# Two-layer hybrid diffusion trunk on one core: adaLN's bias, a fourth weight tile, and the order of the conditioning tiles

## What is computed

```python
def adaln(cvec, w, b):
    m = jax.nn.silu(cvec) @ w + b
    return jnp.split(m[:, None, :], N_MOD, axis=-1)
...
h = modulate(rmsnorm(xp, norm_mix[l]), sh1, sc1)   # h*(1+sc1)+sh1
xp = xp + g1 * mixer(h)
xp = xp + g2 * moe(modulate(rmsnorm(xp, norm_ffn[l]), sh2, sc2))
```

## Time and profile before

| what | us |
|---|---|
| median of 3 runs (1729.19 to 1732.13) | 1731.81 |
| the profiled execution | 1730.03 |
| its span, first to last instruction | 1728.2 |
| PE busy | 1591.8 (92%) |
| DVE busy | 639.7 (37%) |
| ACT busy | 375.8 (22%) |
| POOL busy | 73.6 (4%) |

### The profile page before, as it was taken

One profiled execution on the slowest core, in us unless ns is written; L12 is line 12 of the kernel. 1 busy time (PEld: TensorE's weight loads), 2 busy tenths in 40 slices (PEclk: granted clock), 3 DMA queues, 4 the chain that ended last, 5 costly groups with the idle time before them and its releaser, 6 DMA issues. The chain is left out here.

```text
span 1728.2 us, 23854 instructions
## 1 busy us (share of the span) xinstructions
PE 1591.8 (92%) x9359; PEld 783.6 (45%) x9423; DVE 639.7 (37%) x1350; ACT 375.8 (22%) x700; POOL 73.6 (4%) x118
## 2 busy tenths in 40 slices
PE   4999997999999999999699877889999999999993
PEld 1335546444444444444244345464444444444441
DVE  1124423433333333333315364224333333343333
ACT  1102313112222222221310143121222221221221
POOL 2200000000000000000102033000000000000000
PEclk9999998999999999999899988879999999999996
DMA  9876937799999999998537300178999999999970
GB/s 341 285 292 238 379 104 319 285 399 389 390 389 394 393 399 386 392 382 364 211 136 219 97 13 13 40 304 326 400 383 390 396 395 380 398 392 391 393 293 37
DMA packets 106318, 524.02 MB, mean 303 GB/s; under 512 B 8965, under 2 KB 10160, under 8 KB 54688
## 3 DMA queue, kind: packets, MB, share of 16 engines
q1 hardware_dynamic: 101392, 510.06, 75.5%
q0 software_dynamic: 4880, 13.33, 2.3%
HBM read 518.01 MB, written 2.23 MB: 301 GB/s over the span
## 5 line engine op out<-in xcount | busy, mean ns | idle before, releaser
L903 PE MATMUL bank<-big 128*64 128x512 f32 x2112 | 464.5, 592 | 1.7 <-issue 1.7
L903 PEld LDWEIGHTS bank<-big 128*64 128x64 f32 x2112 | 152.4, 137 | 301.5 <-issue 301.5
L925 PE MATMUL bank<-big 128*64 128x512 f32 x1056 | 241.1, 598 | 1.0 <-DVE big L1526 1.0
L577 PE MATMUL bank<-big,hT 128*128 128x512 f32 (+1 forms) x544 | 233.1, 590 | 7.7 <-ACT hT L1032 5.1
L892 PEld LDWEIGHTS bank<-onehot,big 128*128 128x128 bf16 x3168 | 177.7, 98 | 53.1 <-issue 53.1
L892 PE MATMUL bank<-onehot,big 128*128 128x128 bf16 x3168 | 198.6, 219 | 0.0
L1148 ACT ACTIVATE big<-bank,sl 128x512 bf16<-128x512 f32 x132 | 90.7, 687 | 425.7 <-PE bank L925 425.7
L934 PE MATMUL bank<-big,back 128*128 128x512 bf16 x728 | 171.2, 384 | 9.7 <-DVE big L1544 6.1
L1538 DVE SCALAR_TENSOR_TENSOR xn<-bank,sl,big 128x512 f32<-128x512 f32 x132 | 99.1, 751 | 182.0 <-ACT big L1148 182.0
L577 PEld LDWEIGHTS bank<-big,hT 128*128 128x128 f32 x544 | 104.6, 193 | 133.4 <-issue 123.1
L1518 DVE TENSOR_TENSOR big<-big,bank 128x256 f32<-128x256 f32 x66 | 27.9, 422 | 278.2 <-ACT big L1142 278.2
(11 more groups left out here) (274 smaller groups left out, 1095.5 us busy)
## 6 DMA issues: line engine op xcount, KB each, us to landing
big<-in_w_gate_dram SPq DMA_DIRECT2D x132, 1024.0 KB, 9.3
big<-in_w_up_dram SPq DMA_DIRECT2D x132, 1024.0 KB, 11.2
big<-in_w_down_dram SPq DMA_DIRECT2D x132, 1024.0 KB, 9.0
big<-in_w_ada_dram SPq DMA_DIRECT2D x24, 2048.0 KB, 11.4
big<-in_w_in_rec_dram SPq DMA_DIRECT2D x8, 2048.0 KB, 12.6
big<-in_w_in_attn_dram SPq DMA_DIRECT2D x4, 2048.0 KB, 8.1
big<-in_w_out_attn_dram SPq DMA_DIRECT2D x2, 2048.0 KB, 11.1
big<-in_w_out_rec_dram SPq DMA_DIRECT2D x2, 2048.0 KB, 9.8
```

The costliest lines, as they stand in the source:

```text
L577: mm = pe.matmul(bk[:, 0:w.shape[2]], hT[:, c, g * P:(g + 1) * P], w[:, c, :], start=(c == 0), stop=(c == KC - 1))
L903: mm = pe.matmul(gub[CAP * q:CAP * (q + 1), :], hg[:, j, c, CAP * q:CAP * (q + 1)], gu_slot[2 * j + q][:, :, c, :], start=(c == 0), stop=( ...
L925: mm = pe.matmul(yb[half][CAP * q:CAP * (q + 1), :], hsT[:, f, CAP * q:CAP * (q + 1)], d_slot[2 * j + q][:, f, half * 512:(half + 1) * 512 ...
```

## The change

The bias product goes away, with `dup` and `bias24`. Layer 0's gates get their bias from rows broadcast to all partitions (`brow`, two loads of 1024 values to 128 partitions) when they are evicted; layer 1's kept gates get theirs on DVE instead of ACT's copy; the modulations get theirs from a small table `bmod` (eight loads of 4 KB) by one scalar_tensor_tensor in every ada_mod. Tile 3 gets a place outside the ring (`first4`), so that SP issues it without a wait, and tiles 4, 5 and 6 wait for tiles 0, 1 and 2; from tile 7 on the rule is n-3 as before. The large part of the constants is issued after tile 4 instead of after tile 3. In MID each projection tile goes before its filter job, filtw goes behind the fourth, nab before the fifth and spec behind it. In ATT one ada tile stands ahead of the first scores, each later one comes one unit earlier, and mod and keep move to odd units.

```diff
-    out["dup"] = ...
...
-    MID = [("filt", 0), ("in", 0), ("ada", 4), ("ada", 5)] + [("gate", i) for i in range(4)]
-    MID += [("filt", 1), ("in", 1), ("ada", 6), ("ada", 7), ("mod", 2)]
-    MID += [("filt", 2), ("in", 2), ("ada", 8), ("ada", 9), ("mod", 3), ("filtw", 0), ("filtw", 1)]
-    MID += [("in", 3), ("ada", 10), ("ada", 11)] + [("gate", i) for i in range(4, 8)]
-    MID += [("spec", 0), ("spec", 1), ("spec", 2), ("nab", 0), ("nab", 1), ("in", 4)]
+    MID = [("in", 0), ("filt", 0), ("ada", 4), ("ada", 5)] + [("gate", i) for i in range(4)]
+    MID += [("in", 1), ("filt", 1), ("ada", 6), ("ada", 7), ("mod", 2)]
+    MID += [("in", 2), ("filt", 2), ("ada", 8), ("ada", 9), ("mod", 3)]
+    MID += [("in", 3), ("filtw", 0), ("filtw", 1), ("ada", 10), ("ada", 11)] + [("gate", i) for i in range(4, 8)]
+    MID += [("nab", 0), ("nab", 1), ("in", 4), ("spec", 0), ("spec", 1), ("spec", 2)]
...
-    ATT = []
+    ATT = [("ada", 0)]
     for u in range(NU + 2):
         ATT += [("s", u)] if u < NU else []
         ATT += [("t", u - 1)] if 0 <= u - 1 < NU else []
         ATT += [("v", u - 2)] if 0 <= u - 2 else []
-        ATT += [PAIRS[u // 2 - 1]] if u % 2 == 0 and u >= 2 else []
-        ATT += [("ada", u)] if u < N_ADA else []
+        ATT += [PAIRS[u // 2]] if u % 2 == 1 and u < N_ADA else []
+        ATT += [("ada", u + 1)] if u + 1 < N_ADA else []
...
+        SLOT = [0, 1, 2, 3] + [(n - 4) % 3 for n in range(4, len(order))]
+        BEFORE = [max([m for m in range(n) if SLOT[m] == SLOT[n]], default=None) for n in range(len(order))]
...
-                    if n >= 3 and n - 3 not in early:
-                        sp.wait_ge(mm_done, tile_job[n - 3] + 1)
+                    if BEFORE[n] is not None and BEFORE[n] not in early:
+                        sp.wait_ge(mm_done, tile_job[BEFORE[n]] + 1)
...
-                    if n == 3:
+                    if n == 4:
                         sp.dma_start(cst[:, early_cst:], ...
...
+            for l in range(2):
+                for i, v in enumerate((0, 1, 3, 4)):
+                    pool.dma_start(bmod[:, l, i, :], ...).then_inc(gain_in, 16)
...
             pool.wait_ge(mod_ready, 1)
+            for i, v in enumerate((2, 5)):
+                pool.dma_start(brow[i], row(A["b_ada"][0, v * D:(v + 1) * D], D)).then_inc(brow_in, 16)
+            pool.wait_ge(row_zero, 1)
...
+                    pool.dma_start(bkeep[r:r + G, :], ...).then_inc(bkeep_in, 16)
...
-                    pe.matmul(..., stop=(c >= KC - NT and q > 0))
-                pe.wait_ge(bada_in, 16)
-                pe.wait_ge(cst0_in, 16)
-                pe.matmul(bk[0:ROWS, :], cs("dup", ...), bias24, start=False, stop=True).then_inc(mm_done, 1)
+                    mm = pe.matmul(..., stop=(c >= KC - NT))
+                mm.then_inc(mm_done, 1)
...
-                    if kind == "keep":
-                        bk = take(act, J["keep", u, 1])
-                        act.activation(gsave[r, :], bk[r, :], ACT.Copy).then_inc(ev_done, 1)
...
+                    dve.tensor_tensor(gates[:, g, i // 4, c], bk[:, :], brow[i // 4][:, c], ALU.add).then_inc(ev_done, 1)
...
+                dve.wait_ge(gain_in, 16 * 12)
+                drained(dve, j + 1)
+                link(dve.scalar_tensor_tensor(out=m, in0=m, scalar=float(i % 2), in1=bmod[:, l, i, :]..., op0=ALU.add, op1=ALU.add))
                 if i % 2:
-                    link(dve.tensor_scalar(mod[:, l, i, :, :], mod[:, l, i, :, :], 1.0, None, ALU.add))
...
+                    elif kind == "keep":
+                        dve.tensor_tensor(gsave[r, :], bk[r, :], bkeep[r, :], ALU.add).then_inc(ev_done, 1)
```

More of the change, by code:

```diff
@@ L189, in trunk_kernel @@
         gain = sb("gain", [P, 4, KC])
+        bmod = sb("bmod", [P, 2, 4, KC])
         wr = sb("wr", [P, KC, NE])
@@ L282, in trunk_kernel @@
         cvec_in = sem("cvec_in")
-        bada_in = sem("bada_in")
-        wt_in = [sem(f"wt_in{s}") for s in range(3)]
+        brow_in, bkeep_in = sem("brow_in"), sem("bkeep_in")
+        wt_in = [sem(f"wt_in{s}") for s in range(4)]
         wr_in = sem("wr_in")
@@ L344, in trunk_kernel @@
                 tile_job += [J[f"out{l}"] + 2 * i + 1]
+        SLOT = [0, 1, 2, 3] + [(n - 4) % 3 for n in range(4, len(order))]
+        USE = [SLOT[:n].count(SLOT[n]) for n in range(len(order))]
+        BEFORE = [max([m for m in range(n) if SLOT[m] == SLOT[n]], default=None) for n in range(len(order))]
         def slot(n):
[L347 removed]
+            if SLOT[n] == 3:
+                return first4
+            return wring[:, SLOT[n], :].rearrange("p (c n) -> p c n", c=KC)[:, :, 0:order[n].shape[2]]
         def tile_ready(eng, n):
[L351 removed]
+            eng.wait_ge(wt_in[SLOT[n]], 16 * (USE[n] + 1))
         MB = [[banks[(J[f"pos{l}"] + 1 + i) % 8] for i in range(8)] for l in range(2)]
@@ L488, in _ @@
             pool.wait_ge(mod_ready, 1)
+            for i, v in enumerate((2, 5)):
+                pool.dma_start(brow[i], row(A["b_ada"][0, v * D:(v + 1) * D], D)).then_inc(brow_in, 16)
+            pool.wait_ge(row_zero, 1)
+            for i, v in enumerate((2, 5)):
+                for half in range(2):
+                    r, c = 2 * ROWS * i + ROWS * half, v * D + half * 512
+                    pool.dma_start(bkeep[r:r + G, :], A["b_ada"][1, c:c + 512].unsqueeze(0).to_broadcast([G, 512])).then_inc(bkeep_in, 16)
             pool.dma_start(lmf, A["lmask"]).then_inc(small_in, 16)
@@ L591, in ada_tile @@
                     q = c % NT
-                    pe.matmul(bk[ROWS * q:ROWS * (q + 1), :], cT[:, c, :], w[:, c, :], start=(c < NT), stop=(c >= KC - NT and q > 0))
-                pe.wait_ge(bada_in, 16)
-                pe.wait_ge(cst0_in, 16)
-                pe.matmul(bk[0:ROWS, :], cs("dup", 2 * (N_ADA * l + i), ROWS), bias24, start=False, stop=True).then_inc(mm_done, 1)
+                    mm = pe.matmul(bk[ROWS * q:ROWS * (q + 1), :], cT[:, c, :], w[:, c, :], start=(c < NT), stop=(c >= KC - NT))
+                mm.then_inc(mm_done, 1)
             def ada_mod(i, l):
                 v = (0, 1, 3, 4)[i]
+                pe.wait_ge(cst0_in, 16)
                 drained(pe, J["ada", 2 * v + 1, l])
@@ L1253, in ada_gate @@
                 half, g = i // 2 % 2, i % 2
-                dve.tensor_copy(gates[:, g, i // 4, half * 512:(half + 1) * 512], bk[:, :]).then_inc(ev_done, 1)
+                c = slice(half * 512, (half + 1) * 512)
+                if l == 0:
+                    dve.wait_ge(brow_in, 32)
+                    dve.tensor_tensor(gates[:, g, i // 4, c], bk[:, :], brow[i // 4][:, c], ALU.add).then_inc(ev_done, 1)
+                else:
+                    dve.tensor_copy(gates[:, g, i // 4, c], bk[:, :]).then_inc(ev_done, 1)
             def ada_mod(i, l):
@@ L1261, in ada_mod @@
                     dve.tensor_reduce(mod[:, l, i, 4 * h:4 * h + 4, :], src, AX, ALU.add).then_inc(ev_done, 1)
+                dve.wait_ge(gain_in, 16 * 12)
+                drained(dve, j + 1)
+                m = mod[:, l, i, :, :]
+                link(dve.scalar_tensor_tensor(out=m, in0=m, scalar=float(i % 2), in1=bmod[:, l, i, :].unsqueeze(2).to_broadcast([P, KC, G]),
+                                              op0=ALU.add, op1=ALU.add))
                 if i % 2:
-                    drained(dve, j + 1)
-                    dve.wait_ge(gain_in, 64)
-                    link(dve.tensor_scalar(mod[:, l, i, :, :], mod[:, l, i, :, :], 1.0, None, ALU.add))
                     for g in range(G):
@@ L1404, in attention @@
                         ada_mod(u, 1)
+                    elif kind == "keep":
+                        dve.wait_ge(bkeep_in, 64)
+                        bk = take(dve, J["keep", u, 1])
+                        r = slice(2 * ROWS * u, 2 * ROWS * (u + 1))
+                        dve.tensor_tensor(gsave[r, :], bk[r, :], bkeep[r, :], ALU.add).then_inc(ev_done, 1)
             def add_out(l):
```

14 lines of the change are left out of this document (6 added, 8 removed).

## The result

The changed kernel takes 1735.5 us (median of 18 runs, 1729.43 to 1739.19), the kernel before 1731.09 in the same series (18 runs): a ratio of 1.0024, 95% interval 1.0015 to 1.0034. It is slower by 4.4 us. The forecast of 1727.7 has the wrong sign, and the range ended at 1733.

What follows compares the result with a forecast made beforehand. PE and DMA were taken as close limits in the units, with tiles becoming the bound and early gains carried to the end. 5.8 us gained less 1.7 for clock gave 4.1 less than 1731.8: 1727.7, range 1721 to 1733.

Steps and rivals of the forecast that it cites:

- Projection 1: Layer 0's middle: broadcast rows delay tile 6 by 3.0 us to 65.7; projection starts at 70.9, gain 0.6 us.
- Projection 2: Middle: tile 10 waits for projection 1 and takes 8.0 us; start at 92.9, gain 0.6 us, PE idle 2.2.
- Projection 3: Middle: starts 8.0 us behind projection 2's end instead of 9.05, at 114.9, gain 1.6 us.
- Half tile: Projection 4, behind filter taps, copies, gates and nab: predicted to start at 140.2 us.
- Units: Attention units: start at 157.6, then tiles set the pace at 5.35 us each; tile 28 lands at 213.5.
- the clock term: Waits before projections 2 and 3: one of two followed by half clock, so 1.7 us given back.
- Gain 5.8 us: Attention units: tile 20 issued at 161.1 instead of 164.3, one tile less at the end; transposes start at 223.4.
- rival 5: Units' start: the tile fills PE's idle 3.65 us, tile 20 issued about 2.5 us sooner: 1725.2; chance 0.04.
- Rival 4: PE's new 1.1 us waits in each unit lower its clock there; four such units give 1739; chance 0.09.
- Rival 1: Waits before projections 2 and 3: no half-clock spell, 1726.0, chance 0.17; two spells, 1729.4, chance 0.12.
- Rival 2: PE stays the bound in the units, tiles faster than 5.35 us: 1721.7, or 1723.4 with a spell; chance 0.07.
- rival 3: Units: tiles come more slowly, 5.67 us each, tile 28 2.6 us later: 1730.3 with a spell; chance 0.13.

Runs made afterwards that it cites:

- e1: Kernel before with only the new bias (added at evictions, no bias product), old orders and ring of three: 1726.6 us, 3.8 us less than before.
- e5: e1 with the change's order of the units (ATT), first layer 1 tile behind the wait for the last query eviction: 1730.55 us.
- e12: e1 with layer 1's first ada tile ahead of the query-eviction wait, two useless products behind it, others in the middle's waits: 9.5 us below before.
- e13: The whole change with its first tile ahead of the query-eviction wait and useless products there, in the middle's waits and before the last values: 1723.6 us.
- e3: The change with eleven useless products in PE's waits (middle, before the units, before the last values): 1728.7 us, 1.7 us less than before.
- e11: e1 without the two broadcast row loads, so layer 0's gates lack their bias: 2.6 us less than before, ratio 0.9981.
- e2: The change with a product of zeros put back behind every ada tile: 1735.35 us, ratio 1.0033 to the kernel before.
- e6: e1 with the change's order of MID, the fourth slot and the large constants behind tile 4: 1729.87 us.
- e14: e5 with the first tile ahead of the wait for the last query eviction, no useless product: 4.2 us less than before, ratio 0.9974.
- e7: e1 with the change's order of MID, ring of three, large constants after tile 3: 1729.73 us.

## Why the prediction was wrong

**Most steps on the path held; the clock did not, and the new orders bought nothing.** After's checkpoints, one by one:

- Start: 45.5 against 45.4.
- Projection 1: 2.5 late. Tile 6 came at 66.3 (31.1 + 35.2; 65.7 predicted), and ada 5 ran at half clock (3.49 for 1.92). The prediction had PE wait 2.4 us here (63.3 to 65.7) and priced no spell behind it.
- Projection 2: 3.3 late, those 2.5 and a tile that took 8.8 us instead of 8.0.
- Projection 3: 5.2 late, for projection 2 took 15.67 us. Tile 13 took 8.1.
- Half tile: 6.8 late, by the 1.7 us that projection 3 took longer. The interval between (filter taps, copies, gates: 11.3 us predicted) came out at 11.2. The eviction's row was right too: the gates' add took 0.69 us.
- Units: started 6.8 late, took 67.4 us instead of 65.8. DMA does bind them, as forecast: tile 28 landed at 207.1 + 14.1 = 221.2, and tile 21 at 183.2 (172.6 + 10.6), so 5.4 us each (5.35 predicted). But tile 21 came 7.4 us after tile 20, since its slot waited for a tile run at half clock.
- Transposes to the first expert weights: 35.8 us instead of 32.8, at half clock until about 240 us.

**The step that failed is the clock term.** "I take one of the two as hit: 1.7 us given back". Row by row, half clock lengthened PE's work by 1.6 us (ada 5), 1.7 and 1.7 (projections 2 and 3), 3.05 (the units' first tile, scores and second tile: 8.05 for 5.0) and 3.0 (behind the units), some 11 us in all; the forecast had 1.7, and 1.65 more for the units' first tile. Not all of it lies on the path, since tiles set the pace in the units, but the term was mis-sized in three ways. Both waits were hit, not one. The wait for tile 6 was hit too, and was not on the list. And the two ends of the units were priced too low: at the start the forecast put the tile at half clock but not the scores and the next tile behind it, and the output projection, at full clock before, was taken as fixed. The profiled execution came 8.2 us over its 1725.9, which is 11.4 at the first expert weights less the 1.7 allowed and 1.6 gained behind them.

**A second step, "Gain 5.8 us" in the units, was laid to the wrong cause.** The tile behind the wait was read correctly: rival 5 was rejected for the wait's place, and the 3.65 us stayed (3.91), and half clock was foreseen for it. It freed slot 17 within 2.8 us; tile 20 was issued at 167.2 and not at 161.1 because the units began 6.8 us late. But the gain was not the reordering's. e1, with the old orders, starts the transposes at 224.1, where the forecast had 223.4 for the new ones, and the new order without the early tile (e5) is 4.2 us worse than e1. The middle is alike: with the waits filled, the old order reaches the first scores at 157.2 (e12) and the new one at 158.4 (e13).

The sums of the prediction come out as stated, but for the chance of "faster by over 0.2%": its parts give 0.60, not 0.58.

**Rivals.** Rival 4 had the sign and the cause, half clock from new waits, and the wrong place: it looked inside the units, where the clock was 1.00 and the waits about 1 us. Its 1739 rested on PE running small products between waits; the clock stayed at 2.4 GHz in the changed kernel's units once they were under way. (e1 shows that it need not: one ada tile in its units took 3.62 us behind a wait of 0.99, below.) Rival 1's case of no spell (1726.0, 5.8 us below before) is what e3 makes, 1.7 below. Its first expert weights were issued at 258.2 us, 3.8 earlier than before (5.8 predicted), and from there to the span's end it took 4.2 us longer. Windows 256 to 290 of before and of e3:

```profile
256.00:290.00 34.00, 24.48 (x110) 20.92 (x108) 12.39 (x32) 13.90 (x30) 0.00 (x0) 0.80 0.80 329
```

```profile
256.00:290.00 34.00, 24.82 (x115) 22.85 (x114) 14.24 (x37) 14.02 (x30) 0.00 (x0) 0.70 0.90 370
```

The clock fell from 0.80 to 0.70; 0.1 of 34 us is up to 3.4 of those 4.2. No run was made for that stretch, so its cause is argued only. In any case "what the first 262 us lose or gain is carried to the end" was too simple: from the first expert weights to the span's end the profiled executions took between 1464.6 us (after) and 1470.4 (e3), with 1466.2 before and 1469.2 in e1, though almost everything that was changed lies ahead of that point. Rival 2 did not occur, rival 3 neither: late tiles came every 5.4 us, 382 GB/s over 50 us. The 358 GB/s of the Trainium skill ("DMA: Bandwidth & Descriptors", Specifications) is exceeded here again.

The Trainium skill ("TensorE: Matmul & The Clock Gate", What's actually happening) says that for modelling, the ramp's penalty is below 1% of a typical span. That sentence is on the first rise of the clock; the spells here come back behind one wait after another, and the mean clock of whole executions is 0.960 before and 0.952 after. The difference in the first 262 us, at most 10.8 us, is 0.6% of the span; the change was worth 0.3%, so a term below 1% decided its sign.

## What to carry to other kernels

When work is taken from PE just ahead of a wait for something else, the wait grows by as much, and the work that follows may run at half clock: price that for every wait which the change lengthens, and for the ones at hand-overs it only touches. Work that is ready goes ahead of a wait in program order, and where transfers set the pace, count two things: when the first one of the chain is issued, and how long the way is behind the last. If there is nothing ready, useless products are a cheap test: here they were worth 6 us in the change's orders and nothing that could be told in the old ones. Judge by medians of many runs: the 18 executions of the changed kernel lie between 1729.4 and 1739.2 us, with mean clocks from 0.946 to 0.955, and the change's effect is 4.4.

## What the runs showed of the hardware

What followed a wait did not go by the wait's length alone. Full clock behind idle times of 1.65, 1.79 (e11), 2.10 (e1, tile 6) and 2.22 us (e2, tile 6); half clock behind 2.17 (e6, projection 3), 2.27, 2.95 and 2.98 (after), 2.65 and 2.55 us (e12). The 2.27 came behind transposes of 1.13 us that 0.86 us of idle time preceded. The clock also fell later than the first work behind a wait: in e14 the scores behind 1.78 us ran at full clock and the tile behind them at half, and in e7 the same happened behind 3.92 us. And in e1 one ada tile ran at half clock behind a wait of 0.99 us, where its neighbours behind the same wait took 1.92:

```profile
206.96 3.62 PE L607 MATMUL bank<-big,cT 128*32 128x512 f32 x16 [0.99 <-DMA big<-in_w_ada_dram]
```

No run varied one wait by itself, so no threshold is shown.

Removing 20.6 us of PE work lowered the mean clock of a whole execution from 0.960 to 0.955 in e1 and to 0.952 in the change. In time it gave 3.8 us in e1; the rest was hidden in waits that were there anyway, or came back as slower matmuls.
